# A hybrid encoder step on one Trainium2 core: the first expert pair's rows and the norms behind the experts are done by other engines

## The chip, the cores and the metric

The kernel runs on one core of one Trainium2 chip. The metric is the device time of one execution in microseconds (us); a kernel's time is the median of its runs. One engine each: TensorE (PE in the profile, its weight loads PEld), VectorE (DVE), ScalarE (ACT), GpSimd (POOL), and SyncE (SP), which here only issues DMAs.

## What is computed

One inference step of a two-layer encoder on 256 prompt and 32 sample tokens (T = 288) of width D = 1024. Layer 0 mixes tokens with RWKV-7, layer 1 with forgetting attention; each layer ends with a mixture of 16 experts, of which every token takes two from one group. Each sub-layer is closed by a norm:

```python
x = _layer_norm(ALPHA * x + gt1 * y, p['ln_g'][l, 0], p['ln_b'][l, 0])
h = x * (1 + sc2) + sh2
y = _hmoe(h, p['rg_w'][l], p['rg_b'][l], p['re_w'][l], p['re_b'][l],
          p['exp_wg'][l], p['exp_wu'][l], p['exp_wd'][l])
x = _layer_norm(ALPHA * x + gt2 * y, p['ln_g'][l, 1], p['ln_b'][l, 1])

def _layer_norm(z, g, b):
    mu = jnp.mean(z, -1, keepdims=True)
    var = jnp.mean(jnp.square(z - mu), -1, keepdims=True)
    return (z - mu) * lax.rsqrt(var + LN_EPS) * g + b

def _hmoe(h, comb, wg, wu, wd):   # comb: (token, expert), two weights per token, the rest 0
    hid = jax.nn.silu(jnp.einsum('nd,edf->nef', xf, wg)) * jnp.einsum('nd,edf->nef', xf, wu)
    hid = hid * comb[:, :, None]
    return jnp.einsum('nef,efd->nd', hid, wd)
```

Everything is float32.

## The kernel before

Activations lie feature-major: 8 tiles (KT) of 128 features by 288 tokens. The program of each engine is written out in order, and engines wait for each other through counting semaphores; an engine does nothing past a wait that is not met.

**Order of a layer.** Token mixer, its output projection, `layer_norm(0)` (or 2), `moe`, `layer_norm(1)` (or 3). Norms 0 and 2 are the even ones, norms 1 and 3, behind the experts, the odd ones. After norm 1 TensorE runs `project(4)` (L1118) on the new X; after norm 3 only Y is written out.

**Experts.** The router's choices are turned on DVE into `place` (L1595) and into four selection matrices SEL, one per group of four experts (`select`, L1598). TensorE multiplies SEL with token numbers and weights (`tables(g)`, L960), DVE makes the index table TBL of it (`table(g)`, L1607). Meanwhile the token-major rows `htok` have gone to `hbuf` in HBM (L560). The 16 experts run as 8 pairs of 64 + 64 row slots. The rows of a pair are fetched by GpSimd with an indirect DMA from `hbuf` (`fetch(p)`, L2245) into `xsel[p % 2]`, turned by TensorE (`step_t`, L1010, 8 transposes), copied by ACT to `xselT` (L2000), multiplied with gate and up weights (`step_u`, L1018, 32 instructions for an expert), multiplied by DVE (L1675), turned (`step_h`), copied by DVE (L1678), multiplied with the down weights (`step_d`, L1031, 16 instructions), scaled by DVE into `ysel` and scattered by GpSimd to `zbuf` (L2237).

The first pair is different: `first_rows` (L1001) gathers it with matmuls of `htok` and SEL[0], 8 tiles x 3 token blocks, 48 instructions, straight into the turned form. On TensorE `first_rows`, `tables(0)`, the counts (L1049) and `tables(1)` stand before the first `step_u`; `tables(2)` and `tables(3)` follow the first and second one, and `step_t(1)` the second. GpSimd fetches pairs 1 and 2, then writes the six places scatters (`places`, L2218, L2224), then fetches pair 3, and pair p + 4 once pair p + 2 is turned.

**Expert weights.** 3 MB for an expert, five slots. Five experts are loaded ahead. The rest go through SP in order (L561 to L570): gate/up of expert e + 5 when the gate/up product of e is done, and after each second one the down weights of two, which wait for a down product (`dn_mm`, L566).

**The norm behind the experts.** When all scatters have landed, ACT and SP read both choices of every token back (`rows_back`, L474; halves h = 0 and 1 with semaphores z_in0, z_in1). DVE adds the two choices in four quarters of 256 features (L1734 for two blocks of 128 tokens, L1735 for the last 32 tokens). TensorE transposes each tile (3 instructions of L628, two of 128 tokens and one of 32), DVE forms Z = ALPHA x + gate y from it (`residual`, L1479, L1492), ACT squares Z (L1964). In the odd norms GpSimd adds up Z (L2200), and TensorE adds the squares itself: `add_squares` (L923, two instructions of 288 columns) for tile k - 2 behind the transposes of tile k. In the even norms DVE adds up Z (L1486) in `residual` and GpSimd the squares, and TensorE has four matmuls at the end, one pair on each sum and on each last tile. The mean is read by ACT (L1966); DVE centers (L1507) beside GpSimd (L2205), makes the reciprocal deviation (L1516 to L1518) and scales.

**Filler.** `spin(bank, n)` (L630) runs n matmuls of 288 columns whose result nobody reads (each is two instructions, float32).

## Time and profile before

| | us |
|---|---|
| median of 3 runs | 1046.03 |
| lowest, highest | 1041.26, 1055.11 |
| the profiled execution | 1048.08 |
| its span, first to last instruction | 1046.4 |
| TensorE busy | 917.7 |
| DVE, ACT, GpSimd busy | 327.6, 232.0, 177.2 |

The profile is of one execution. Its times are counted from the start of the span. "Busy" of TensorE counts pipelined matmuls and is not work at the peak. The chain is the work that ended last, followed back from the last instruction.

### The profile page before, as it was taken

The numbers are of one execution on the slowest core, as the hardware profiler recorded it, in microseconds if no ns is written. First come the engines' busy times: TensorE is split into PE (matmuls) and PEld (weight loads), VectorE is DVE, ScalarE is ACT, GpSimd is POOL, SyncE is SP. The second block draws the span as 40 slices with busy tenths as digits, with TensorE's granted clock in tenths as the row PEclk, the third lists the DMA queues.
The fourth block names the chain that finished last, engine by engine and source line by source line (L and its number), as shares of the span: only waits on it lengthen the run. The fifth ranks groups of instructions, "written<-read, shape, count | busy, mean of one in ns | idle before, by whom it ended". The sixth has DMA issues, their size and how long they took to land.

```text
span 1046.4 us, 19214 instructions
## 1 busy us (share of the span) xinstructions
PE 917.7 (88%) x8268; PEld 627.0 (60%) x8268; DVE 327.6 (31%) x841; ACT 232.0 (22%) x528; POOL 177.2 (17%) x230
## 2 busy tenths in 40 slices
PE   2799999889988989999787899898899989997874
PEld 0477667869876757655354567554467757553442
DVE  0523341535425454211123301221221354211134
ACT  0312225223215041111001332221222131110004
POOL 0100002011542151221031110000000233211122
PEclk9899989999998998999996999899889998999996
DMA  9742221340246931799959454555646724899931
GB/s 385 322 152 89 81 81 48 127 163 4 85 173 271 387 139 57 277 425 423 424 194 369 194 189 179 195 196 214 243 164 234 322 97 182 328 424 421 383 110 46
DMA packets 28773, 230.14 MB, mean 220 GB/s; under 512 B 6590, under 2 KB 7006, under 8 KB 13552
## 3 DMA queue, kind: packets, MB, share of 16 engines
q1 hardware_dynamic: 19200, 208.66, 49.8%
q0 software_dynamic: 7776, 15.50, 4.2%
q10 hardware_dynamic: 1712, 4.75, 1.3%
q8 instruction: 66, 1.08, 0.4%
q14 instruction: 19, 0.16, 0.0%
HBM read 222.16 MB, written 16.32 MB: 228 GB/s over the span
## 4 chain that ended last, share of the span: by engine, by line
PE 68%; DMA 19%; DVE 5%; issue 3%; ACT 2%; POOL 1%; SPq 1%; ACTq 0%; POOLq 0%; DVEq 0%
PE ps L646 21%; PE ps L984 10%; DMA arena<-in_w 8%; DMA arena<-in_experts 6%; PE ps L772 5%; PE ps L667 5%; PE ps L1040 4%; PE ps L628 3%; PE ps L779 3%; DMA arena<-zbuf 2%; PE ps L1005 2%; DMA ring<-in_w 2%; PE ps L1154 2%; PE ps L970 1%; PE ps L925 1%
## 5 line engine op out<-in xcount | busy, mean ns | idle before, releaser
L646 PE MATMUL ps<-arena,ring 128*128 128x288 f32 x896 | 230.9, 420 | 11.5 <-DVE arena L1471 3.8
L646 PEld LDWEIGHTS ps<-arena,ring 128*128 128x128 f32 x896 | 173.9, 196 | 68.9 <-issue 17.1
L984 PE MATMUL ps<-arena 128*64 128x256 f32 x960 | 118.6, 404 | 18.0 <-DMA arena<-in_experts 12.6
L984 PEld LDWEIGHTS ps<-arena 128*64 128x64 f32 x960 | 75.0, 146 | 60.8 <-DMA arena<-in_experts 17.8
L667 PE MATMUL ps<-arena,csil 128*32 128x512 f32 x256 | 40.1, 756 | 36.8 <-DMA arena<-in_w 36.8
L772 PE MATMUL ps<-arena 64*64 64x64 f32 x1888 | 63.8, 221 | 4.3 <-issue 3.2
L772 PEld LDWEIGHTS ps<-arena 64*64 64x64 f32 x1888 | 60.3, 137 | 10.2 <-issue 8.5
L628 PEld LDWEIGHTS ps<-con,arena 128*128 128x128 f32 (+3 forms) x270 | 34.5, 149 | 45.5 <-issue 26.6
L628 PE MATMUL ps<-con,arena 128*128 128x128 f32 (+3 forms) x270 | 52.5, 309 | 10.2 <-DVEq L1737 6.3
L1040 PE MATMUL ps<-arena 128*64 128x512 f32 x208 | 58.4, 598 | 0.8 <-DVE arena L1678 0.8
L2003 ACT ACTIVATE arena<-ps 128x128 f32<-128x128 f32 x36 | 10.0, 277 | 208.8 <-PE ps L984 208.8
L633 PE MATMUL ps<-con 128*128 128x288 f32 x170 | 43.1, 408 | 2.1 <-DVE arena L1682 2.1
L1678 DVE COPY arena<-ps 128x128 f32<-128x128 f32 x36 | 10.5, 292 | 107.9 <-PE ps L628 107.6
L1931 ACT ACTIVATE arena<-ps 128x512 f32<-128x512 f32 x44 | 26.2, 597 | 79.2 <-PE ps L772 59.0
L1868 ACT ACTIVATE arena<-ps 128x288 f32<-128x288 f32 x40 | 16.1, 407 | 124.3 <-PE ps L646 124.3
L667 PEld LDWEIGHTS ps<-arena,csil 128*32 128x32 f32 x256 | 7.7, 125 | 58.1 <-issue 31.8
L1682 DVE TENSOR_SCALAR arena<-ps,TBL 128x512 f32<-128x512 f32 x32 | 22.6, 747 | 62.4 <-PE ps L1040 62.4
L1964 ACT ACTIVATE arena<-arena 128x288 f32<-128x288 f32 x32 | 14.2, 443 | 124.5 <-DVEq L1496 124.5
L633 PEld LDWEIGHTS ps<-con 128*128 128x128 f32 x170 | 31.8, 190 | 12.3 <-issue 3.9
L2237 POOL DMA_INDIRECT zbuf<-arena,TBL x16 | 16.1, 1005 | 127.5 <-DVE arena L1682 127.5
L1492 DVE SCALAR_TENSOR_TENSOR arena<-ps,mod,arena 128x256 f32<-128x256 f32 x64 | 20.6, 364 | 48.8 <-PE ps L646 36.8
L1315 DVE SCALAR_TENSOR_TENSOR arena<-arena,vec 128x288 f32<-128x288 f32 x48 | 21.6, 515 | 45.0 <-PE ps L646 44.0
(306 smaller groups left out, 1270.3 us busy)
## 6 DMA issues: line engine op xcount, KB each, us to landing
arena<-in_experts SPq DMA_DIRECT2D x30, 2048.0 KB, 20.6
ring<-in_w SPq DMA_DIRECT2D x24, 2048.0 KB, 8.4
arena<-in_w SPq DMA_DIRECT2D x16, 2048.0 KB, 13.3
arena<-in_experts SPq DMA_DIRECT2D x30, 1024.0 KB, 19.3
ring<-in_experts SPq DMA_DIRECT2D x6, 2048.0 KB, 19.8
ring<-in_experts SPq DMA_DIRECT2D x6, 1024.0 KB, 16.5
arena<-in_lora SPq DMA_DIRECT2D x1, 2560.0 KB, 40.8
hbuf<-arena SPq DMA_DIRECT2D x4, 512.0 KB, 3.2
```

Of the source, the lines that this page charges most:

```text
L628: return nc.tensor.transpose(out, in_, ident[0:n, 0:n])
L633: mm(ps[:, bank, 0:T], ident, con[:, 0:T], start=True, stop=True)
L646: last = mm(ps[:, tile % 4, 0:T], wslot[j][:, k, o * P:(o + 1) * P], rhs_at(k), start=k == 0, stop=k == KT - 1)
L667: last = mm(ps[32 * q:32 * q + 32, ADA_BANK[turn], :], c2[:, 2 * j + k, :], w[:, k, q, :], start=j == 0 and k == 0, stop=j == ADA_TURN - 1 ...
L772: last = mm(o, lhs[r, k, :], rhs[r, k, :], start=True, stop=True)
L779: last = mm(ps[r, bank, k * 64:(k + 1) * 64], lhs[r, k, :], rhs[r, k, :], start=n == 0, stop=n == len(terms) - 1)
L984: last = mm(ps[64 * j:64 * j + 64, 2 + b, 0:256], x(k), ewgu[slot][:, k, j * 256:(j + 1) * 256], start=k == 0, stop=k == KT - 1)
L1005: last = mm(ps[:, k // 4, k % 4 * P:(k % 4 + 1) * P], htok[0:n, i, k * P:(k + 1) * P], SEL[0][0:n, i * 4 * C:i * 4 * C + 2 * C], start=i = ...
L1040: last = mm(ps[HALF[b], 4 + n, :], hidT[b][:, f * C:(f + 1) * C], ewd[(2 * p + b) % NSLOT][:, f, n * 512:(n + 1) * 512], start=f == 0, sto ...
L1315: last = V.scalar_tensor_tensor(cut((11 + n % 3) * ACOL + k * T, T), XX[:, k, :], v(f"mu{i}", k), Hh[:, k, :], ALU.mult, ALU.add)
L1682: return V.tensor_scalar(y, ps[:, 4 + b, :], w.bitcast(F32), None, ALU.mult)
L1931: ins = Ac(B[dst], src, ACT.Copy, scale=-1.0 if product == "Bt" else 1.0)
```

## The change

1. `first_rows` is gone. Pair 0 is fetched like the others; `xsel` and `xselT[0]` move into the place of `htok`, `ysel` to a place of its own. On TensorE the two groups of table products and the counts come first, then three filler matmuls and `step_t(0)`; `step_t(1)` stands before the second `step_u` instead of behind it. GpSimd fetches pairs 0 and 1, writes the places, then fetches 2 and 3.
2. In the odd norms DVE adds the first two quarters of the choices and GpSimd the other two; DVE adds up Z in `residual`, GpSimd adds up the squares, and TensorE's end is that of the even norms.
3. The filler before the transposes of the odd norms (24 matmuls) and before `project(4)` (5) is gone.

```diff
-            ysel = [cut(at_rows + n * D, D) for n in range(2)]
-            xselT = [take(D) for _ in range(2)]
-            xsel = [ring[:, ECOL + n * D:ECOL + (n + 1) * D] for n in range(2)]
+            xsel = [cut(at_rows + n * D, D) for n in range(2)]
+            xselT = [cut(at_rows + 2 * D, D), take(D)]
+            ysel = [take(D) for _ in range(2)]
...
@@ TensorE, layer_norm and moe @@
-                if n % 2:
-                    add_squares(n, KT - 2)
...
-                if not n % 2:
-                    pe.wait_ge(s["ln_ssum"], n // 2 + 1)
-                    mm(ps[:, 5, 0:T], co("mean"), ssum, start=True, stop=False)
-                add_squares(n, KT - 1).then_inc(s["ln_var"], 1)
+                pe.wait_ge(s["ln_ssum"], n + 1)
+                mm(ps[:, 5, 0:T], co("mean"), ssum, start=True, stop=False)
+                pe.wait_ge(s["ln_sq"], KT * (n + 1))
+                mm(ps[:, 5, 0:T], co("mean"), acts(SQB[n])[:, KT - 1, :], start=False, stop=True)\
+                    .then_inc(s["ln_var"], 1)
...
-                pe.wait_ge(s["sel_ready"], 4 * layer + 1)
-                first_rows()
                 tables(0)
                 for i, n in enumerate(TOK):
                     last = mm(ps[:, 7, 448:464], ones[0:n, :], mask[0:n, i, :], start=i == 0, stop=i == 2)
                 last.then_inc(s["cnt_mm"], 1)
                 tables(1)
+                spin(2, 3)
+                step_t(0)
                 for e in range(NE):
                     step_u(e)
                     if e < 2:
                         tables(2 + e)
                     if e:
                         step_h(e - 1)
-                    if e == 1:
-                        step_t(1)
-                    if e % 2 == 0 and e:
+                    if e % 2 == 0:
                         if e + 2 < NE:
                             step_t(e // 2 + 1)
-                        step_d(e // 2 - 1)
+                        if e:
+                            step_d(e // 2 - 1)
...
-                spin(6, 24)
                 for k in range(KT):
                     c = layer * KT + k
                     if k % 2 == 0:
-                        pe.wait_ge(s["zsum"], 4 * layer + k // 2 + 1)
+                        pe.wait_ge(s[("zsum", "zsum2")[k // 4]], 2 * layer + k % 4 // 2 + 1)
...
                     last.then_inc(s["zt_mm"], 1)
-                    if k > 1:
-                        add_squares(2 * layer + 1, k - 2)
...
-            spin(6, 5)
             project(4, lambda k: X[:, k, :], ...)
@@ DVE, residual @@
                 for k in range(KT):
-                    if k > 1 and not n % 2:
+                    if k > 1:
                         did(V.tensor_tensor(zsum_, Z[:, 0, :] if k == 2 else zsum_, Z[:, k - 1, :], ALU.add))
@@ DVE, moe @@
-                for q in range(4):
+                dve.wait_ge(s["z_in0"], 48 * (layer + 1))
+                for q in range(2):
                     c = slice(q * 256, (q + 1) * 256)
-                    dve.wait_ge(s[f"z_in{q // 2}"], 48 * (layer + 1))
@@ ACT, moe @@
                 step_t(0)
                 for e in range(NE):
                     step_u(e)
-                    if e == 1:
-                        step_t(1)
-                    if e % 2 == 0 and 0 < e < NE - 2:
+                    if e % 2 == 0 and e + 2 < NE:
                         step_t(e // 2 + 1)
@@ GpSimd, layer_norm and moe @@
             def layer_norm(n):
-                total, x, ready, done = (zsum_, Z, "z_ready", "ln_sum") if n % 2 else (ssum, Q, "ln_sq", "ln_ssum")
+                if n % 2:
+                    pool.wait_ge(s["z_in1"], 48 * (layer + 1))
+                    for q in range(2, 4):
+                        c = slice(q * 256, (q + 1) * 256)
+                        ch.did(Pl.tensor_tensor(zin[:, 0:2, 0, c], zin[:, 0:2, 0, c], zin[:, 0:2, 1, c], ALU.add))
+                        ch.link(Pl.tensor_tensor(zin[0:TS, 2, 0, c], zin[0:TS, 2, 0, c], zin[0:TS, 2, 1, c], ALU.add))
+                        pool.sem_inc(s["zsum2"], 1)
                 for k in range(1, KT - 1):
-                    pool.wait_ge(s[ready], KT * n + k + 1)
-                    ch.link(Pl.tensor_tensor(total, x[:, 0, :] if k == 1 else total, x[:, k, :], ALU.add))
-                pool.sem_inc(s[done], 1)
+                    pool.wait_ge(s["ln_sq"], KT * n + k + 1)
+                    ch.link(Pl.tensor_tensor(ssum, Q[:, 0, :] if k == 1 else ssum, Q[:, k, :], ALU.add))
+                pool.sem_inc(s["ln_ssum"], 1)
...
                 def fetch(p):
                     pool.wait_ge(s["tbl_ready"], 4 * layer + p // 2 + 1)
-                    if p > 2:
+                    if p >= 2:
                         pool.wait_ge(s["xt_mm"], 2 * (p0 + p - 1))
...
-                for p in range(1, 3):
+                for p in range(2):
                     fetch(p)
                 places()
-                fetch(3)
+                for p in range(2, 4):
+                    fetch(p)
```

## Rows read from the trace of the kernel before

**Rows 1.** the page's part 4, chain by engine, share of the span.

```profile
PE 68%; DMA 19%; DVE 5%; issue 3%; ACT 2%; POOL 1%; SPq 1%; ACTq 0%; POOLq 0%; DVEq 0%
```

**Rows 2.** the chain in order of time, first layer's experts: start us, us, what.

```profile
397.85 8.51 PE ps L1005 x48
...
406.36 1.70 PE ps L970 x12
...
411.94 5.40 PE ps L984 x32
...
425.09 1.09 ACT arena L2000 x2
...
426.27 5.10 PE ps L984 x32
431.37 1.13 PE ps L628 x9
...
440.28 3.67 PE ps L984 x32
```

**Rows 3.** timeline, second layer's experts: start us, us, engine, line, operation [idle before].

```profile
857.33 8.51 PE L1005 MATMUL ps<-arena 128*128 128x128 f32 x48 [0.20 <-DVE arena L1602]
...
870.39 6.60 PE L984 MATMUL ps<-arena 128*64 128x256 f32 x32
```

**Rows 4.** timeline of SP's queue behind the first down product, both layers.

```profile
436.13 1.45 SPq L540 DMA_DIRECT2D arena<-in_experts  x2
...
894.35 0.80 SPq L540 DMA_DIRECT2D arena<-in_experts  x2
```

**Rows 5.** the chain in order of time, end of the first layer's expert loads.

```profile
487.30 30.52 DMA arena<-in_experts
```

**Rows 6.** windows: us, each engine's busy us, TensorE clock, DMA share, GB/s.

```profile
409.00:412.00 3.00, 3.00 (x15) 2.92 (x16) 0.98 (x2) 0.00 (x0) 1.14 (x1) 0.50 0.12 15
432.00:434.00 2.00, 2.00 (x13) 0.89 (x13) 0.15 (x1) 1.08 (x2) 0.63 (x1) 1.00 0.02 6
```

**Rows 7.** timeline of the norms behind the experts, first and second layer.

```profile
556.47 0.69 DVE L1734 TENSOR_TENSOR arena<-arena 128x512 f32<-128x512 f32 x1 [12.65 <-DMA arena<-zbuf]
...
561.13 0.64 DVE L1492 SCALAR_TENSOR_TENSOR arena<-ps,mod,arena 128x256 f32<-128x256 f32 x2 [0.16 <-DVE arena L1735]
562.01 0.64 DVE L1492 SCALAR_TENSOR_TENSOR arena<-ps,mod,arena 128x256 f32<-128x256 f32 x2 [0.24 <-DVE arena L1492]
...
576.27 0.41 ACT L1966 ACTIVATE lnw<-ps 128x288 f32<-128x288 f32 x1 [2.74 <-PE ps L916]
...
1014.89 0.69 DVE L1734 TENSOR_TENSOR arena<-arena 128x512 f32<-128x512 f32 x1 [13.06 <-DMA arena<-zbuf]
...
1031.05 0.41 ACT L1966 ACTIVATE lnw<-ps 128x288 f32<-128x288 f32 x1 [0.86 <-PE ps L916]
```

**Rows 8.** groups by form, DVE and GpSimd: busy us, mean ns | idle before.

```profile
L1492 DVE SCALAR_TENSOR_TENSOR arena<-ps,mod,arena 128x256 f32<-128x256 f32 x32 | 15.5, 484 | 48.8 <-PE ps L646 36.8 <-PE ps L628 10.5 <-DVE arena L1492 1.2
...
L1486 DVE TENSOR_TENSOR lnw<-lnw,arena 128x288 f32<-128x288 f32 x10 | 4.6, 459 | 2.5 <-DVE arena L1492 2.5
...
L2163 POOL TENSOR_TENSOR arena<-arena,con 128x512 f32<-128x512 f32 x5 | 6.4, 1271 | 4.9 <-DVE arena L1400 4.8
L2224 POOL DMA_INDIRECT tbl<-ENT,SLOT x12 | 11.6, 967 | 7.1 <-DVEq L1640 4.1 <-issue 3.1
```

**Rows 9.** timeline of GpSimd, the first gather of the first layer.

```profile
409.96 1.14 POOL L2232 DMA_INDIRECT ring<-hbuf,TBL  x1 [20.11 <-DVEq L1617]
```

**Rows 10.** the gathers' line L2232, issue to landing.

```profile
DMA to landing us min/median/max: 2.7/6.3/14.8
```

**Rows 11.** the centering adds' line L1507 on DVE, duration ns min/median/max.

```profile
L1507 DVE TENSOR_TENSOR arena<-arena,lnw x20: 394/453/1051, 375.0 to 1037.3; 128x288 f32<-128x288 f32 x20
```

**Rows 12.** the chain in order of time, the projection behind the first layer.

```profile
582.72 5.81 PE ps L646 x16
...
628.22 31.05 PE ps L646 x128
```

More of the change, by code:

```diff
@@ L455, in build @@
             xt_act hid_ready ht2_mm ht2_ready dn_mm y_dve z_scat0 z_scat1 o_in0 o_in1 o_in2 o_in3 oidx o_idx o_gath0 o_gath1 o_xt_mm o_xta o_gu o_silu o_hid o_ht_mm o_ht o_dn
-            o_ydve o_scat o_over z_in0 z_in1 zsum zt_mm zt_free
+            o_ydve o_scat o_over z_in0 z_in1 zsum zsum2 zt_mm zt_free
             fw_in attn_small f_mm f_act f_neg f_scan nf_ready kv_out logf_out g_in0 g_in1 att_mm att_dve att_act
@@ L972, in tables @@
                     last.then_inc(s["sel_mm"], 1)
+                tables(0)
+                for i, n in enumerate(TOK):
+                    last = mm(ps[:, 7, 448:464], ones[0:n, :], mask[0:n, i, :], start=i == 0, stop=i == 2)
+                last.then_inc(s["cnt_mm"], 1)
+                tables(1)
                 def rows_in(x, b):
@@ L999, in moe @@
                 n0, p0 = layer * NE, layer * NPAIR
[L1001 to L1008 removed]
                 def step_t(p):
[L1012 removed]
+                    pe.wait_ge(s[f"gath{p % 2}"], 16 * ((p0 + p) // 2 + 1))
                     for k in range(KT):
@@ L1043, in step_d @@
                     last.then_inc(s["dn_mm"], 1)
-                pe.wait_ge(s["sel_ready"], 4 * layer + 1)
-                first_rows()
-                tables(0)
-                for i, n in enumerate(TOK):
-                    last = mm(ps[:, 7, 448:464], ones[0:n, :], mask[0:n, i, :], start=i == 0, stop=i == 2)
-                last.then_inc(s["cnt_mm"], 1)
-                tables(1)
+                spin(2, 3)
+                step_t(0)
                 for e in range(NE):
```

12 lines of the change are left out of this document (removed).

## Prediction

> **What bounds the kernel now.** I read the chain by engine first: TensorE holds two thirds of it, DMA a fifth [rows 1]. A change pays where TensorE, or what feeds it, is late, and each stage is read for itself. In each layer the change touches the start of the experts and the norm behind them.
>
> The start of the experts, first layer, as the chain in order of time has it [rows 2]: at 397.85 DVE's choices are there and TensorE gathers the first pair's rows by matmul (48 instructions, 8.51 us). Behind it come the table products of group 0 (1.70), then the counts and the products of group 1 (408.06 to 411.94, 3.88), and only then the first gate/up. So 14.1 us stand between the choices and the first expert. In the second layer it is 857.33 to 870.39, 13.1 us [rows 3], which leaves 2.85 for the counts and group 1.
>
> Behind it, DMA. The loads for freed slots go through SP in order, and after two of them SP waits for the first down product: its next load goes out at 436.13, and at 894.35 in the second layer [rows 4]. The end of the stage is a load that stands 30.52 us in the queue, until 517.82 [rows 5]; but just before 436 the DMA engines had run dry, with a share of 0.02 at 432 to 434 [rows 6]. So all later loads queue behind that first down product, and the stage's end moves with it: what counts is the stretch from 397.85 to 436.1 (38.2 us) and 857.33 to 894.3 (37.0).
>
> The norm behind the experts, read in the timeline: DVE adds the two choices from 556.47, takes the first tile at 561.13, and ACT reads the mean at 576.27, 19.8 us after the start; second layer 1014.89 to 1031.05, 16.2 us [rows 7]. DVE's tiles waited 10.5 us in all for the transposes (L628) [rows 8]: between one tile's transposes and the next TensorE adds a tile of squares.
>
> **Part one: the first pair.** Removed: 8.51 us from the front. Behind the choices now come group 0 (1.70), counts and group 1 (2.85 to 3.88) and six filler instructions of 288 columns, 0.24 each as in the projection (31.05/128 [rows 12]), 0.49 at 1.2 GHz. The clock is 0.50, so 1.2 GHz, at 409 to 412, just behind the small products [rows 6]. TensorE is through 6.0 to 8.5 us after the choices. Beside it runs the new chain: group 0 done at 1.7; from the end of that product (408.06) to the issue of GpSimd's gather (409.96 [rows 9]) 1.9, DVE's table in it; then the landing, 2.7 us after issue at best, 6.3 in the median, 14.8 at worst [rows 10]. The long ones ran beside expert loads; here none runs, since the first is released by the first gate/up, so I take 2.7 to 3.7: rows there at 6.3 to 7.3. Both chains meet near 7.3. Then eight transposes, about 1.0 (nine in 1.13), twice that at 1.2 GHz, and ACT's second copy, 0.54 (two in 1.09) and 0.2 of hand-over [rows 2]. The first gate/up starts 9 to 12 us after the choices; I take 10.
>
> The first gate/up took 5.40 and 6.60; at full clock it is 3.67 [rows 2, 3]. The excess, 1.73 and 2.93, is 3.5 and 5.9 us at half speed. Filler and transposes are now dense work ahead of it, so the clock should be back somewhat earlier in it: 5.2. It ends at 15.2 instead of 19.5 and 19.6: 4.3 us gained per layer.
>
> From there to the first down product the same instructions run in another order. The second pair's transposes ahead of the second gate/up hide ACT's copy, 1.2 us bare before (425.06 to 426.27), but uncover the hidden block's turn and DVE's copy, for which ACT's 0.54 and a transpose of 0.13 are the nearest rows, with hand-overs 0.8 to 1.1: 0.1 to 0.4 gained, none counted beyond 0.1. In the first layer the third gate/up took 5.10 instead of 3.67 [rows 2], behind that 1.2 us hole; I count half of the 1.43. Together 5.0 and 4.3 us (bounds 2 and 6.5 each). From SP's load behind the down product on, the shift is carried in full.
>
> Queues. GpSimd now issues two gathers, then six places scatters (0.97 each [rows 8], some 7.5 us with gaps), and then the gathers of pairs 2 and 3, which used to stand before the scatters or wait for later transposes. The scatters start some 8 us earlier than before, with DVE's entries, so pair 2's gather goes out about 18 us after the choices and is read at about 29: 10 us of room against a median of 6.3; free, and some 4 us at the worst landing. Pair 1's is read at 17 and issued at 5. Its bytes, at most 128 rows of 4 KB (0.5 MB, about 1 us), fall ahead of the first down product, where DMA runs dry anyway. SP's order is unchanged.
>
> **Part two: the norm behind the experts.** DVE had 4.66 us for four quarters (556.47 to 561.13); two are 2.33. GpSimd adds the other two: 1.27 for a 128x512 add [rows 8] and no more than that for the small piece, so 4 to 5 us in all, and DVE needs them only at its fifth and seventh tile: hidden. But the engines hold each other up: DVE's centering adds took 453 ns in the median and up to 1051, beside GpSimd's of the same stretch [rows 11]. I take 3.0 for DVE's two quarters (2.3 to 3.8). The Trainium skill (GPSIMD Engine Reference, Key points) says that GpSimd shares its SBUF interfaces with VectorE and contends with DVE instructions that have two SBUF inputs. That speaks against this change, whose adds on both engines are such; the trace agrees with the 1051.
>
> Then eight tiles on DVE, 0.88 each (561.13 to 562.01 [rows 7]), from the third on with a running add of Z, 0.46 less some overlap [rows 8]: 2 x 0.88 + 6 x 1.3 + 0.1 = 9.7. TensorE has one tile's transposes to do in that time (about 0.4, or 0.7 at 1.2 GHz), so DVE leads. The last tile is ready 12.7 us after the start, the mean is read 0.8 to 1.3 later: 13.9. Gained 19.8 - 13.9 = 5.9 and 16.2 - 13.9 = 2.3 us (within 1.5 each way). GpSimd's squares follow each tile and are not slower than DVE; the last two matmul pairs of the variance stand behind the mean as in the first norms.
>
> The filler goes too. The 24 pairs hid behind the DMA: free by itself. But TensorE comes to the projection with a hole behind it. There the first tile's 16 instructions took 5.81, against 3.9 at full clock [rows 12]; all at 1.2 GHz they take 7.8. I charge 1.0 us (0 to 2.5, the rest for tiles behind). No matmul follows the last norm. The projection's weights are asked for at the landing, 20 us ahead.
>
> **Sum:** -5.0 - 4.3 - 5.9 - 2.3 + 1.0 = -16.5 us. The profiled execution took 1048.08 (span 1046.4), so 1031.6 by it; it lies 2 us above the median shown, 1046.03, which gives 1029.5. I say 1030.5.
>
> **Rivals.**
> (a) All at its good end: clock kept through the tables, rows there after 2.7 us, no hold-up on DVE: -6 and -5.5 at the experts, -6.5 and -3.5 in the norms, projection free, some -22: 1024.5. For: each piece has a row; against: the first gate/up was slowed by the clock in both layers. 0.14.
> (b) The first gather lands like the median one, 6.3: first gate/up at 12.6 in both layers, 2.6 later each: 1036. For: no cover but the filler; against: empty queues. 0.10.
> (c) DVE and GpSimd hold each other up at every add: ten adds of DVE in each norm take 0.6 more, 12 us in all: 1042. For: the 1051; against: the squares start just behind DVE's running add. 0.08.
> (d) Slower, by the clock. Place: from the tables to the end of the second gate/up. Small products and a wait stand where dense matmuls stood; if 1.2 GHz then lasts through both gate/ups, a layer pays 2.5 (start at 12.5), 2.0 (first gate/up 7.2), 1.7 (group products), 1.0 (transposes) and 3.7 (second gate/up), 10.9, and two of them 21.8: 1052. It turns the sign from 16.5 us on, some 33 us of additional lower clock. For: 0.50 at 409 to 412. Against: dense work brought the clock back after 3.5 and 5.9 us. 0.05. The Trainium skill (TensorE: Matmul & The Clock Gate, What's actually happening) calls the throttled state the default that activity releases; by that rule taking filler out invites (d). The trace bears out the fall, not a long stay.
>
> **How the numbers follow.** The sum has 0.63. The range, 1022 to 1041, takes in (a), (b) and the near half of (c). Faster by over 2% (below 1025.1) are most of (a) and the sum's lower tail: 0.18; slower by over 2% is only a worse (d): 0.02; within 2%: 0.80. 2% is about what a measurement of this kernel can tell from no change.
>
> **What would show it.** Right: first gate/up about 10 us after the choices, no 48-matmul group; SP's load behind the first down product about 33 us after the choices in both layers; the mean about 14 us after DVE's first add in both norms, its tiles no longer waiting for L628. Wrong: pair 0's transposes waiting for the gather beyond 8 us; DVE adds of 0.7 us and more all along; a projection whose first tile takes 8 us.

## The result, and the profile after

The changed kernel takes 1043.03 us (median of 20 runs, 1033.78 to 1054.06) beside 1048.91 us for the kernel before on the same chip (20 runs, 1038.59 to 1057.76). The ratio is 0.9935, with a 95% interval from 0.991 to 0.996: 6.8 us less (4.2 to 9.4). The ratio, here and below, goes by the fast runs, those not more than 1.5% above the fastest of their kernel. Forecast were 16.5 us less, 1030.5 us, with a range from 1022 to 1041; the measured time lies outside it. The sign was right and the size 2.4 times too large.

The profiled execution has a span of 1041.5 us (before 1046.4). Its chain by engine stands as before, TensorE two thirds and DMA a fifth, with a little more for DVE [rows 1]:

```profile
PE 66%; DMA 19%; DVE 7%; issue 4%; ACT 2%; POOL 1%; SPq 1%; ACTq 0%; POOLq 0%; DVEq 0%
```

Timeline of TensorE in the changed kernel, first layer's expert start (start us, us, engine, line, operation, [idle before]); against [rows 2]:

```profile
398.72 2.39 PE L961 MATMUL ps<-VAL,arena 128*128 128x6 f32 x12 [0.36 <-DVE arena L1580]
401.04 1.57 PE L967 MATMUL ps<-arena,con 128*128 128x16 f32 x6
402.54 3.00 PE L961 MATMUL ps<-VAL,arena 128*128 128x6 f32 x12
405.47 3.25 PE L630 MATMUL ps<-con 128*128 128x288 f32 x6
408.51 1.66 PE L625 MATMUL ps<-con,arena 128*128 128x128 f32 x8
410.95 3.67 PE L981 MATMUL ps<-arena 128*64 128x256 f32 x32 [0.78 <-ACT arena L1979]
...
425.01 3.67 PE L981 MATMUL ps<-arena 128*64 128x256 f32 x32 [1.22 <-DVE arena L1656]
```

The 48-matmul group is gone. TensorE never waits between the choices (398.72) and the transposes of pair 0 (408.51): its own small products and fillers fill 9.8 us, and the first gate/up starts 12.2 us after the choices, not 10. In the second layer (choices at 854.81) the transposes start after 8.8 us and the gate/up after 10.8. The windows say why (us, PE busy, PEld, DVE, ACT, POOL, TensorE clock, DMA share, GB/s):

```profile
398.00:400.00 2.00, 1.64 (x10) 1.24 (x9) 1.54 (x2) 0.00 (x0) 0.00 (x0) 0.88 0.00 0
404.00:406.00 2.00, 2.00 (x8) 1.92 (x8) 0.39 (x2) 0.00 (x0) 1.17 (x2) 0.50 0.32 84
408.00:410.00 2.00, 2.00 (x10) 1.65 (x8) 1.64 (x12) 0.39 (x1) 0.00 (x0) 0.56 0.05 20
410.00:412.00 2.00, 1.22 (x12) 0.91 (x12) 1.73 (x9) 1.98 (x3) 1.21 (x2) 1.00 0.01 4
```

The stretch at 1.2 GHz, about 409 to 415 before ([rows 6] show its start), has moved ahead to the tables. Twelve table instructions that take 1.77 at full clock take 3.00 there, and a filler instruction 0.54. The first gate/up itself ran at full clock, 3.67 us in both layers.

What counts is SP's load behind the first down product, in both layers; against [rows 4]:

```profile
433.44 1.03 SPq L537 DMA_DIRECT2D arena<-in_experts  x2
...
889.90 0.88 SPq L537 DMA_DIRECT2D arena<-in_experts  x2
```

It comes 34.7 and 35.1 us after the choices (398.72; 854.81), where it was 38.2 and 37.0: 3.5 and 1.9 us gained of 5.0 and 4.3 forecast. (Below, "+55.3" is a time behind the start of the norm's reciprocal ahead of the experts, which each profile has: norm 0's in the first layer, norm 2's in the second.) In the second layer the third gate/up ran into a second stretch at 1.2 GHz, which the first layer was spared:

```profile
880.00:882.00 2.00, 2.00 (x16) 1.48 (x14) 0.00 (x0) 0.00 (x0) 0.00 (x0) 0.70 1.00 424
882.00:884.00 2.00, 2.00 (x13) 1.36 (x11) 0.00 (x0) 0.00 (x0) 0.00 (x0) 0.50 0.84 338
```

The norm behind the first layer's experts, timeline, against [rows 7]:

```profile
553.52 1.26 POOL L2177 TENSOR_TENSOR arena<-arena 128x512 f32<-128x512 f32 x1 [9.39 <-DMA arena<-zbuf]
553.79 1.54 DVE L1713 TENSOR_TENSOR arena<-arena 128x512 f32<-128x512 f32 x1 [13.50 <-DMA arena<-zbuf]
554.75 1.16 POOL L2178 TENSOR_TENSOR arena<-arena 32x256 f32<-32x256 f32 x1
555.25 0.93 DVE L1714 TENSOR_TENSOR arena<-arena 32x256 f32<-32x256 f32 x1
...
556.33 1.56 DVE L1713 TENSOR_TENSOR arena<-arena 128x512 f32<-128x512 f32 x1 [0.15 <-DVE arena L1714]
...
557.82 0.94 DVE L1714 TENSOR_TENSOR arena<-arena 32x256 f32<-32x256 f32 x1
...
558.91 0.64 DVE L1470 SCALAR_TENSOR_TENSOR arena<-ps,mod,arena 128x256 f32<-128x256 f32 x2 [0.16 <-DVE arena L1714]
...
570.21 0.41 ACT L1945 ACTIVATE lnw<-ps 128x288 f32<-128x288 f32 x1 [1.02 <-PE ps L910]
...
570.93 1.17 PE L915 MATMUL ps<-arena,con 128*128 128x288 f32 x2
...
572.70 0.94 DVE L1495 TENSOR_SCALAR lnw<-lnw 128x288 f32<-128x288 f32 x1
573.68 1.95 DVE L1496 RECIPROCAL lnw<-lnw 128x288 f32<-128x288 f32 x1
```

DVE's two quarters take 5.12 us (553.79 to 558.91), more than its four did (4.66): an add of 128x512 takes 1.54 beside GpSimd's instead of 0.69. The mean is read 16.4 us after DVE's start, not 13.9. In norm 3 DVE starts at 1011.38 and the mean is read at 1026.17, after 14.8. GpSimd's half of the rows landed first there, and its first add started 1.6 us before DVE's.

Behind the mean, norm 1 lost another 0.74 us: its reciprocal starts 3.47 us after the mean is read, where it was 2.73. The same stretch before, same view:

```profile
576.07 0.65 PE L925 MATMUL ps<-arena,con 128*128 128x288 f32 x2
...
578.53 0.43 DVE L1517 TENSOR_SCALAR lnw<-lnw 128x288 f32<-128x288 f32 x1
```

In the changed kernel TensorE's last pair of products for the variance stands behind the mean's. At half clock it takes 1.17 us. Then DVE's next instruction starts 0.2 us later, and the one behind it (L1495) takes 0.94 instead of 0.43. Of the 30 norms behind experts with this end in the profiles, 21 have the pair at 1.16 or 1.17 and the reciprocal 3.46 to 3.48 after the mean; the other nine have it at 1.00 or less and 2.71 to 2.73.

For what follows I count stages from the start of one norm's reciprocal to the next one's. "Load" is SP's load behind the first down product, "add" the first add of the choices on either engine.

| us | before | after |
|---|---|---|
| layer 0: reciprocal of norm 0 to load | 58.8 | 55.3 |
| to add | 179.2 | 175.4 |
| add to reciprocal of norm 1 | 22.5 | 20.2 |
| reciprocal of norm 1 to that of norm 2 | 256.9 | 259.6 |
| layer 1: reciprocal of norm 2 to load | 58.4 | 56.6 |
| to add | 179.0 | 176.5 |
| add to reciprocal of norm 3 | 18.9 | 19.2 |

The fourth line holds the attention, which the change doesn't touch. Over the later profiles it lies between 253.9 and 269.5 us, so its scatter alone is larger than the effect looked for.

### The profile page after: what moved, and what is told of

Same layout as the page of the kernel before. It is cut to its first block, busy times and chain, and to the rows that moved or that the text cites. A ratio compares the mean times of both kernels' runs of the same rounds, so it can differ in the third digit from the quotient of the medians.

```text
span 1041.5 us, 18838 instructions
## 1 busy us (share of the span) xinstructions
PE 879.5 (84%) x8070; PEld 598.6 (57%) x8070; DVE 333.3 (32%) x845; ACT 232.0 (22%) x528; POOL 187.6 (18%) x240
## 4 chain that ended last, share of the span: by engine, by line
PE 66%; DMA 19%; DVE 7%; issue 4%; ACT 2%; POOL 1%; SPq 1%; ACTq 0%; POOLq 0%; DVEq 0%
PE ps L643 21%; PE ps L981 9%; DMA arena<-in_w 8%; DMA arena<-in_experts 6%; PE ps L769 5%; PE ps L664 5%; PE ps L1028 4%; PE ps L625 3%; PE ps L776 3%; DMA arena<-zbuf 2%; DMA ring<-in_w 2%; PE ps L961 2%; PE ps L1132 2%; PE ps L782 1%; PE ps L925 1%
## 5 line engine op out<-in xcount | busy, mean ns | idle before, releaser
L643 PE MATMUL ps<-arena,ring 128*128 128x288 f32 x896 | 230.3, 419 | 13.4 <-ACT arena L1953 5.3
L643 PEld LDWEIGHTS ps<-arena,ring 128*128 128x128 f32 x896 | 173.6, 196 | 71.0 <-issue 19.2
L981 PEld LDWEIGHTS ps<-arena 128*64 128x64 f32 x960 | 75.7, 143 | 61.3 <-issue 19.7
L625 PE MATMUL ps<-con,arena 128*128 128x128 f32 (+3 forms) x398 | 69.3, 305 | 39.9 <-DVEq L1716 36.0
L625 PEld LDWEIGHTS ps<-con,arena 128*128 128x128 f32 (+3 forms) x398 | 48.1, 150 | 74.8 <-DVEq L1716 37.8
L1028 PE MATMUL ps<-arena 128*64 128x512 f32 x208 | 58.4, 598 | 0.8 <-DVE arena L1656 0.8
L1656 DVE COPY arena<-ps 128x128 f32<-128x128 f32 x36 | 10.5, 292 | 107.9 <-PE ps L625 107.6
L1910 ACT ACTIVATE arena<-ps 128x512 f32<-128x512 f32 x44 | 26.2, 597 | 78.2 <-PE ps L769 59.1
L1132 PE MATMUL ps<-arena,ring 128*128 128x288 f32 x128 | 33.4, 415 | 0.0
L1979 ACT ACTIVATE arena<-ps 128x512 f32<-128x512 f32 x36 | 19.7, 595 | 51.9 <-PE ps L625 43.9
## 6 DMA issues: line engine op xcount, KB each, us to landing
arena<-in_w SPq DMA_DIRECT2D x16, 2048.0 KB, 13.5
arena<-in_experts SPq DMA_DIRECT2D x30, 1024.0 KB, 19.2
```

The lines of the kernel that those rows point to most:

```text
L625: return nc.tensor.transpose(out, in_, ident[0:n, 0:n])
L643: last = mm(ps[:, tile % 4, 0:T], wslot[j][:, k, o * P:(o + 1) * P], rhs_at(k), start=k == 0, stop=k == KT - 1)
L981: last = mm(ps[64 * j:64 * j + 64, 2 + b, 0:256], x(k), ewgu[slot][:, k, j * 256:(j + 1) * 256], start=k == 0, stop=k == KT - 1)
L1028: last = mm(ps[HALF[b], 4 + n, :], hidT[b][:, f * C:(f + 1) * C], ewd[(2 * p + b) % NSLOT][:, f, n * 512:(n + 1) * 512], start=f == 0, sto ...
L1132: last = mm(ps[:, b, 0:T], wslot[j][:, k, o * P:(o + 1) * P], X[:, k, :], start=k == 0, stop=k == KT - 1)
L1910: ins = Ac(B[dst], src, ACT.Copy, scale=-1.0 if product == "Bt" else 1.0)
```

## The experiments

The first four split the change in its halves, undid GpSimd's share, and put the fillers back. Each was timed (12 runs) beside the kernel before (1049.57 us, 35 runs).

**e1: the expert half alone.** All hunks of the expert start in `moe` (pair 0 fetched, the new order on TensorE and GpSimd), none of the norms'.

> The expert half of the change alone; both later norms stay as before. Theory S (the shifts read at the four stages of the profile after: -3.5 and -1.9 us at the loads behind the first down product, -2.6 and -1.3 us at the reciprocals of norms 1 and 3): 4 to 5.5 us under before, ratio 0.995 to 0.996. Rival T (what the experts gain is given back behind the last load, where the tails of both layers were about 1 us longer): 1 to 2 us under before, ratio 0.998 to 0.999.

Measured: ratio 0.9952 (0.9908 to 0.9996), 5.0 us less. The stages repeat: load at +55.2 and +57.0, add at +175.7 and +178.3. Theory S stands in the middle; T's range (1 to 2 us) lies inside the interval (0.4 to 9.7) too. Its norms, as before in code, took 22.5 and 22.4 us. So the 18.9 us of norm 3 in the profile before was the one short norm of four, with a granted clock of 0.68 over the 16 us from the first add:

```profile
1015.00:1031.00 16.00, 12.51 (x43) 7.89 (x44) 9.09 (x24) 3.54 (x8) 4.75 (x6) 0.68 0.01 2
```

and here 0.57 over 20 us:

```profile
1015.00:1035.00 20.00, 16.12 (x44) 9.81 (x44) 9.12 (x24) 3.90 (x9) 4.76 (x6) 0.57 0.00 0
```

That the old norm goes by TensorE's clock is read from these rows, not tested; the changed one took 19.0 to 19.9 us in norm 3 in every profile with this end.

**e2: the norm half alone.** All hunks of the norms and fillers, the expert start as before.

> The norm half alone (GpSimd adds two quarters and the squares, DVE the tiles, TensorE no squares and no filler products); the experts start as before. Theory S: 3 to 4 us under before, ratio 0.996 to 0.997, with DVE's two quarters in norm 1 again at 4 to 5 us beside GpSimd's. Rival N (the norms gain nothing, the whole 6.8 us is the experts'): within 1 us of before, ratio 0.999 to 1.001.

Measured: 0.9994 (0.9962 to 1.0026), 0.6 us less. The profile has norm 1 at 20.2 us, so its gain of 2.4 is there, and DVE's two quarters at 1.47 and 1.56 for the large adds. In time rival N is nearer, though theory S's 3 to 4 us still lie inside the interval, at its end. The profile's loads behind the first down product stood at +60.9 and +63.5, 2 and 5 us later than before, in a part that this edit doesn't touch.

**e3: DVE adds all four quarters.**

```diff
@@ TensorE @@
-                        pe.wait_ge(s[("zsum", "zsum2")[k // 4]], 2 * layer + k % 4 // 2 + 1)
+                        pe.wait_ge(s["zsum"], 4 * layer + k // 2 + 1)
@@ DVE @@
-                dve.wait_ge(s["z_in0"], 48 * (layer + 1))
-                for q in range(2):
+                for q in range(4):
                     c = slice(q * 256, (q + 1) * 256)
+                    dve.wait_ge(s[f"z_in{q // 2}"], 48 * (layer + 1))
@@ GpSimd, layer_norm: its two quarters gone @@
...
```

> The changed kernel with all four quarters of the two expert choices added by DVE; GpSimd keeps the squares. Theory C (DVE and GpSimd hold each other up in these adds, so that the share given to GpSimd is worth almost nothing): DVE's adds go back to 0.69 and 0.41 us, two quarters take 2.3 us and four 4.7 us, the whole within 1 us of the changed kernel. Rival A (the share was worth its whole price, four quarters of DVE being late for the transposes of tiles 4 to 7): 1.5 to 4 us slower than the changed kernel.

Measured: 1041.17 us, 0.9929 (0.9888 to 0.997). Its norm 1, DVE's timeline:

```profile
551.46 0.69 DVE L1713 TENSOR_TENSOR arena<-arena 128x512 f32<-128x512 f32 x1 [12.98 <-DMA arena<-zbuf]
552.07 0.40 DVE L1714 TENSOR_TENSOR arena<-arena 32x256 f32<-32x256 f32 x1
...
556.12 0.48 DVE L1470 SCALAR_TENSOR_TENSOR arena<-ps,mod,arena 128x256 f32<-128x256 f32 x1 [0.16 <-PE ps L625]
...
570.14 1.95 DVE L1496 RECIPROCAL lnw<-lnw 128x288 f32<-128x288 f32 x1
```

The adds are back at 0.69 and 0.40, four quarters take 4.66 us, and the reciprocal starts 18.7 us after the first add instead of 20.2 (norm 3: 18.3 instead of 19.2). Theory C holds, and more than it said: in its stage the share given to GpSimd is a loss. From the first add to the reading of the mean it is 15.96 us instead of 16.69. That is 0.7 us of the 1.5; the other 0.75 is the step behind the mean described above, whose long form this execution was spared in both norms. In the later profiles with this edit (e10 to e12) norm 1 has the long form again and takes 19.4, against 20.2. Rival A falls by the stage; the two ratios, 0.6 us apart with an interval of some 5 us either way, can't tell it.

**e4: the fillers back.** `spin(6, 24)` ahead of the transposes and `spin(6, 5)` ahead of `project(4)`.

> The changed kernel with both fillers back (24 products ahead of the transposes of the later norms, 5 ahead of the projection behind norm 1); its output is the same. Theory P (the change's norm is slower than forecast partly because TensorE stands at half clock through norms 1 and 3): start to reciprocal of norm 1 falls by 1 to 2 us, and the kernel by 1 to 3 us. Rival D (the norm goes at DVE's pace and TensorE's clock doesn't matter there): within 0.7 us of the changed kernel.

Measured: 1039.92 us, 0.9918 (0.9883 to 0.9952). The fillers do hold the clock up to the norm, but not in it. Windows of e4:

```profile
552.00:554.00 2.00, 0.00 (x0) 0.00 (x0) 0.94 (x1) 0.00 (x0) 1.17 (x1) 1.00 0.19 36
556.00:560.00 4.00, 3.22 (x13) 1.69 (x12) 3.36 (x7) 0.51 (x2) 1.78 (x2) 0.50 0.99 418
```

and of the changed kernel:

```profile
552.00:554.00 2.00, 0.00 (x0) 0.00 (x0) 0.21 (x1) 0.00 (x0) 0.48 (x1) 0.50 0.16 43
556.00:560.00 4.00, 2.92 (x11) 1.68 (x11) 3.44 (x6) 0.20 (x1) 2.39 (x2) 0.50 1.03 422
```

Norm 1 took 20.2 us and norm 3 19.2, to 0.02 us what they were: theory D in the norm, since the fillers left the clock in it as it was. The time, 1.8 us less by the two ratios, is nearer to theory P's 1 to 3 us, but within the intervals.

The next four looked at the expert start, with one execution each, profiled; one of the kernel before beside them took 1051.64 us. Their times can't be told from chance; what they say is in their rows.

**e5: pair 1's transposes behind the second gate/up again.**

```diff
-                    if e % 2 == 0:
+                    if e == 1:
+                        step_t(1)
+                    if e % 2 == 0 and e:
...
@@ ACT: its copies in the same order @@
```

> The changed kernel with the transposes of pair 1 behind the second gate/up product, where they stood before. Theory Q (moving them ahead of it is what costs the second layer 1.3 us between the second gate/up product and the first down product, and their signal comes 4 us late): second load's release falls by about 1 us in both layers (from +43.7 and +43.4 us behind the reciprocal to about +42.7), the load behind the first down product by 0.5 to 1.5 us (from +55.3 and +56.5). Rival W (the order of the two is worth nothing, what counts is the sum of TensorE's work up to the first down product): that load stays within 0.3 us in layer 0.

The second load goes out at +42.9 and +42.7 as expected, but the load behind the first down product at +57.8 and +57.4, later than in the changed kernel: the third gate/up fell into 1.2 GHz in both layers (6.32 and 6.10 us, 3.67 at full clock). The changed kernel has such loads too where its clock falls there (+57.1 to +57.8 in e4, e9, e13 and e14), so the later load is the clock's and not shown to be the order's. Theory Q's gain isn't seen; the order gives 0.8 us at the second load and nothing behind it. The kernel took 1042.13 us.

**e6: ten fillers behind the first tables.** `spin(2, 5)` behind `tables(0)`, none ahead of `step_t(0)`.

> The changed kernel with ten filler products directly behind the first tables and none ahead of the transposes of pair 0. Theory K (the first gate/up product was late because TensorE's clock stood at half from the tables to the first transposes, though TensorE was busy): the granted clock rises earlier, the first expert load is released 1 to 2 us earlier than +38.0. Rival G (the gather's rows set that point): release within 0.4 us of +38.0. If the clock stays at half all the same, the fillers cost 2 us.

The first load goes out at +37.5 and +38.5. The ten fillers took 5.17 us at half clock; the clock came back by the second tables and fell again. Behind the second gate/up TensorE stood idle three times with nothing in the profile that it waited for ("issue"); from 420 to 426 the DMA share was 0.67 to 0.79:

```profile
421.25 0.48 PE L961 MATMUL ps<-VAL,arena 128*128 128x6 f32 x3 [0.24 <-issue]
422.67 0.48 PE L961 MATMUL ps<-VAL,arena 128*128 128x6 f32 x3 [0.94 <-issue]
424.08 0.81 PE L961 MATMUL ps<-VAL,arena 128*128 128x6 f32 x6 [0.94 <-issue]
```

The load behind the first down product came at +59.1 and +59.9, the kernel took 1053.4. Theory K falls as a cure: filling by hand at this place cost more than it gave in this profile.

**e7: no filler ahead of pair 0's transposes.** `spin(2, 3)` dropped.

> The changed kernel without the six filler products ahead of the transposes of pair 0. If the gather's rows set the start (rival G): transposes start at the same 10.0 us behind the choices, first gate/up slower by 0 to 2 us from a longer time at half clock. If TensorE's own work set it: transposes start 0.3 to 2 us earlier.

```profile
404.80 3.00 PE L961 MATMUL ps<-VAL,arena 128*128 128x6 f32 x12
408.72 1.97 PE L625 MATMUL ps<-con,arena 128*128 128x128 f32 x8 [0.92 <-DMA arena<-hbuf,TBL]
```

Here TensorE does wait for the gather, 0.92 us, and the transposes start 7.7 us after the choices (400.99) instead of 9.8. So the rows are there at 7.7, and in the changed kernel TensorE's own work set the start. But the first gate/up then ran partly at half clock (5.67 us), the first load went out at +38.0 and +38.3 as before, and the next ones at +57.8 and +57.9. What the start gained (1.8 us at the first gate/up), the clock took. (The kernel's 1056.34 us has 268 us between the reciprocals of norms 1 and 2, which this edit doesn't touch.)

**e8: the first hidden rows turned ahead of the tables of pairs 6 and 7.** The 1.22 us wait of the third gate/up for DVE's L1656 (first timeline above) is DVE's copy standing behind `table(3)`.

```diff
@@ TensorE @@
-                    if e < 2:
-                        tables(2 + e)
+                    if e == 0:
+                        tables(2)
                     if e:
                         step_h(e - 1)
+                    if e == 1:
+                        tables(3)
@@ DVE: the same, table(3) behind step_h(0) @@
```

> The changed kernel with the transpose and the copy of the first hidden rows ahead of the tables of pairs 6 and 7, on TensorE and on DVE. Theory H (TensorE's wait of 1.2 us ahead of the third gate/up product, which DVE's copy of the hidden rows ends behind the table's four instructions, sets the first down product): the load behind the first down product 1 to 1.5 us earlier, at about +54.2 and +55.3. Rival: DVE's copy was hidden by something else that is late, and the load stays within 0.3 us.

Measured: load at +53.8 and +53.5, the kernel 1036.84 us. The wait is gone, the third gate/up took 3.67 in both layers and no second stretch at 1.2 GHz follows in either. At the load the first layer gained the 1.5 us of theory H; the second gained 3.1, the wait and the clock. At the first add of the choices it is 1.9 and 1.5 us: of the second layer's gain only half had arrived by then, in this one execution.

Then four timed kernels, beside the kernel before (1048.81 us, 29 runs).

**e9: the changed kernel again.**

> The changed kernel itself, beside the three that follow: 0.992 to 0.995 of before; first add to reciprocal 20.2 us in norm 1 and 19.2 in norm 3 again if these are set by the engines' pace. Of the load behind the first down product a second reading: +55.3 us (layer 0) where the third gate/up product runs at full clock, +57 where the clock falls under it.

1041.73 us, 0.9936 (0.9892 to 0.998): the result repeats. Norms 20.2 and 19.8. The load came at +57.3 in the first layer, with the third gate/up mostly at half clock (6.59 us), and at +54.0 in the second, at full clock. Expected were +57 and +55.3. Here the first expert load went out at +36.5 and +36.1, 1.5 and 1.9 us earlier than in the first profile (see the last section), about what the +54.0 is early. Windows of the first layer:

```profile
424.00:426.00 2.00, 0.78 (x5) 0.60 (x7) 1.34 (x6) 0.00 (x0) 0.00 (x0) 0.71 0.98 340
426.00:430.00 4.00, 4.00 (x20) 2.40 (x19) 0.00 (x0) 0.00 (x0) 0.00 (x0) 0.50 0.96 370
```

**e10: e3 and e8 together.**

> The changed kernel with DVE adding all four quarters and the first hidden rows turned ahead of the tables of pairs 6 and 7. Theory C+H (both edits act where they were seen to act): load behind the first down product +53.8 and +53.5 us, first add to reciprocal 18.7 and 18.3 us, in all 4 to 6 us under the changed kernel. Rival: the stretch behind the last load grows by what the start gains (it did by about 1 us in each layer), and the whole is 1.5 to 3 us under the changed kernel.

1039.13 us, 0.9912 (0.9874 to 0.995). The load at +53.0 and +52.7, the third gate/up without a wait:

```profile
422.74 0.33 PE L625 MATMUL ps<-con,arena 128*128 128x128 f32 x1
422.91 1.67 PE L961 MATMUL ps<-VAL,arena 128*128 128x6 f32 x12
424.51 3.67 PE L981 MATMUL ps<-arena 128*64 128x256 f32 x32
```

Reciprocal to reciprocal is 192.7 and 193.4 us, against 198.8 and 195.4 of e9 on the same chip, 8 us by the stages, 2.6 by the medians (the intervals overlap). Part of the 8 is not the edits': e9's first layer had its third gate/up at half clock. Against the first profile the load is 2.4 and 3.9 us earlier, of which some 1.5 in each layer is the earlier first load that e9 has too; at the first add of the choices 2.2 and 1.4 us are left. In the second layer the stretch from the load to the add is 122.4 us, the longest of all, so the rival is not excluded.

**e11: e10 with both groups of fillers.**

> The kernel e10_both with the two groups of fillers back. With GpSimd adding, the fillers kept the clock at full up to the norm and yet left norm 1 at 20.2 us, since DVE and GpSimd set its pace. Theory D (DVE's 1.25 us a tile sets the pace here too, whatever the clock): norms 18.7 and 18.3 us, within 1 us of e10_both. Rival P (with the adds short, TensorE's transposes and mean products at half clock are what is left): norms 0.5 to 1.5 us shorter each.

1035.21 us over 6 runs, 0.9881 (0.9826 to 0.9935): the lowest median of the study, 12.5 us below the kernel before by the ratio. The norms are 19.4 and 19.0 us where e10 had 19.4 and 18.3, so theory D holds in them and P's shorter norms are not seen; the kernel, though, is 3.9 us below e10 by the medians, not within 1 us, with overlapping intervals. What the fillers may give is behind norm 1: the projection's first tile took 4.72 us in e11,

```profile
575.03 4.72 PE ps L643 x16
```

6.89 in e10 and 5.62 in the changed kernel:

```profile
576.38 6.89 PE ps L643 x16
```
```profile
577.41 5.62 PE ps L643 x16
```

and its x128 group starts 48.1 us behind the reciprocal in e11, 50.3 in e10. In e4, though, the first tile took 6.25 with the same fillers; that they always help is not shown.

**e12: the norm half alone with DVE adding all quarters.** e2 with the edit of e3.

> The norm half alone with DVE adding all four quarters (squares by GpSimd, sum of tiles by DVE, no squares and no fillers on TensorE); the experts start as before. Theory C: first add to reciprocal 18.7 us in norm 1 (before 22.5) and 18.3 in norm 3 (before 18.9 or, at half clock, 22.4), so 4 to 7 us under before, ratio 0.993 to 0.996. Rival R (what the norm half gains is lost at the experts, where the norm half alone showed its loads 2 to 5 us late in both layers): within 1.5 us of before.

1052.01 us, 1.0000 (0.9955 to 1.0046). The profile has norms of 19.4 and 19.0 us, and loads at +59.0 and +56.9, so rival R's late loads are not seen in the stages (this execution has 269.5 us between the reciprocals of norms 1 and 2). The time is nearer to what R said, within 1.5 us of before; a gain of 4 us is still in the interval, one of 7 is not.

**e13, e14, e15: a known delay at each place.** The stages promise more than the times give. So 13 instructions whose result changes nothing went ahead of DVE's quarters in norm 1 (e13) and norm 3 (e14), and 40 small ones ahead of the choices of layer 0 (e15). The kernel before took 1052.38 us beside them (29 runs), and the three 1052.43, 1052.87 and 1051.77 (12 runs each).

```diff
+                if layer == 0:
+                    for _ in range(13):
+                        link(V.tensor_tensor(zin[:, 0:2, 1, 0:256], zin[:, 0:2, 1, 0:256], zin[:, 0:2, 1, 0:256], ALU.max))
```

> The changed kernel with 13 idle instructions on DVE (each the greater of a value and itself) ahead of its first quarter of the choice in norm 1, about 10 us by 0.7 to 0.8 us each. Theory F (a microsecond at norm 1 is one of the whole): the time grows by the delay less what GpSimd's half and the transposes lose nothing by, 8 to 10 us over the changed kernel, 1.002 to 1.004 of before. Rival A (the stages behind wait for loads that were issued ahead of the norm): 3 to 7 us, and reciprocal of norm 1 to reciprocal of norm 2, 256 to 259.6 us in the changed kernel, falls by the rest.

> The same delay in norm 3, behind which only the output follows. Both theories: the time grows by the delay seen at the reciprocal of norm 3, 8 to 10 us over the changed kernel. It is the measure for the other two.

> The changed kernel with 40 idle instructions on DVE ahead of the choices of layer 0, about 10 us by 0.25 us each. Theory F (the loads behind the first down product are bound by the DMA queues from there to the last load, so the whole shifts): the first down product's load, the read of the rows and the time are all later by the delay, 9 to 11 us. Rival B (the loads already under way fill part of it, or the tail behind the last load shrinks): the read of the rows is later by 2 us less than the load.

| | seen in its stage, us later than the changed kernel | ratio to before (interval) | time over the changed kernel |
|---|---|---|---|
| e13 | reciprocal of norm 1: 29.0 - 20.2 = 8.9 | 1.0025 (0.9993 to 1.0057) | 9.4 |
| e14 | reciprocal of norm 3: 29.0 less 19.0 to 19.9 = 9.1 to 10.0 | 1.0014 (0.9983 to 1.0046) | 8.3 |
| e15 | load: 67.8 less 55.2 to 57.8 = 10.0 to 12.6 | 1.0029 (0.9995 to 1.0063) | 9.9 |

(The last column is the ratio less 0.9935, times 1048.9.) A microsecond at each of the three places is about one of the whole, with some 4 us either way on each time. Theory F fits all three. Rival B falls: in e15 the read of the rows was late by as much as the load (10.2 to 13.5 us at the first add). Rival A is not excluded: e13's profile has 253.9 us between the reciprocals of norms 1 and 2, the shortest of all, 2 to 6 us less than the changed kernel's 256.0 and 259.6, as A expects; but that execution was the fastest of e13's 12, 5 us below their median, and the median shows no such gift. In e13 DVE's delay itself was 12.0 us and only 8.9 of it reached the reciprocal, because GpSimd was through when DVE's quarters came:

```profile
553.24 11.98 DVE L1713 TENSOR_TENSOR arena<-arena 128x512 f32<-128x512 f32 x13 [13.65 <-DMA arena<-zbuf]
565.25 0.69 DVE L1716 TENSOR_TENSOR arena<-arena 128x512 f32<-128x512 f32 x1
...
566.41 0.69 DVE L1716 TENSOR_TENSOR arena<-arena 128x512 f32<-128x512 f32 x1 [0.15 <-DVE arena L1717]
```

Alone, the two quarters take 2.3 us: 2.8 of the 5.12 are the hold-up by GpSimd.

## Why the prediction was wrong in size

The forecast had the places and the direction right. Three terms failed: the small products and fillers ahead of the first gate/up, the missing wait ahead of the third one, and DVE's two quarters.

**Start of the experts, -5.0 and -4.3: found -3.5 and -1.9.** The step "TensorE is through 6.0 to 8.5 us after the choices" failed; it took 9.8 us (8.8 in the second layer). I had priced the fillers at both clocks, but group 0, the counts and group 1 at their rows of before, 1.70 and 2.85 to 3.88, read behind 48 dense matmuls and partly at full clock. In the changed kernel the small products themselves stand at 1.2 GHz: 2.39 + 1.57 + 3.00, and 3.25 for the fillers (1.77 + 1.22 + 3.00 + 3.25 in the second layer, where the clock fell a little later). So the first load went out 17.4 and 16.4 us after the choices (416.14; 871.24) instead of 19.5 and 19.7: 2.1 and 3.3 us gained of 4.3. The gather was sized almost rightly (rows there at 7.7 in e7, 6.3 to 7.3 forecast), as was its queue: pair 2's went out at 418.13, 19.4 us after the choices (18 forecast), and nothing waited for it. The first gate/up was forecast at 5.2 us, partly at half clock; the rows have it at 3.67, all at full clock, and yet SP's load went out 5.2 and 5.7 us behind its start. That the forecast number came out is luck: by these rows the clock wasn't its cause, and what the cause was is open.

The second part of the miss is "none counted beyond 0.1" between the first gate/up and the first down product. The new order has a wait of 1.22 us of its own ahead of the third gate/up, for DVE's copy behind `table(3)`, in place of the one for ACT. From the first load to the one behind the first down product it took 17.3 us in the first layer (before 18.8), with the third gate/up at full clock, and 18.7 in the second (before 17.3), with it at 5.36 us: 1.4 gained, 1.3 lost. Over seven profiles with this start (the first, e1, e3, e4, e9, e13, e14) the load lies at +55.2 to +57.8 in the first layer and, with e15's second layer, at +54.0 to +57.3 in the second; with the old one over three (before, e2, e12) at +58.8 to +60.9 and +56.9 to +63.5. Rival (d) named the clock over the small products rightly; that it would stay low through both gate/ups, and so its price, not. Ten fillers ahead of the second group didn't cure it (e6).

**From the load on "the shift is carried in full": right in the main.** In the first layer the add came 3.8 us later before than after, 2.5 in the second; in e15, whose load was 10.0 to 12.6 later, it came 10.2 to 13.5 later (188.8 less 175.3 to 178.6). The stretch from load to add itself scatters, from 118.2 to 121.3 us in the first layer and from 119.5 to 122.4 in the second over all profiles, so a shift of 1 to 2 us can't be followed through it.

**Norm 1, -5.9: found -3.4 at the mean, -2.4 at the reciprocal. Norm 3, -2.3: found -1.4 at the mean and +0.3 at the reciprocal.** (The mean is counted from DVE's first add, as in the forecast, the reciprocal from the first add on either engine.) The step that failed is "I take 3.0 for DVE's two quarters (2.3 to 3.8)". They took 5.12 and 3.87. In e13, where they took 2.3 and GpSimd had long finished its adds, the mean was read 13.3 us after the first of them, so the rest of the sum up to the mean stood. What norm 1 gained less at its reciprocal than at its mean is 0.3 us for GpSimd's earlier start and 0.74 for the end: "the last two matmul pairs of the variance stand behind the mean" is in the forecast, but priced at nothing. In norm 3 that end cost nothing in this profile (2.72 both times), and the 1.6 us between GpSimd's start and DVE's make the difference. Rival (c) was this mechanism with the wrong reach: it put 0.6 us on ten adds, and the runs show 0.85 on a large and 0.5 on a small add of the quarters and nothing on the tiles. There the argument against (c) held. DVE's running add (L1464) is over when GpSimd starts to add the square (L2183), and GpSimd works beside DVE's tile, which takes one operand from PSUM; all three keep their pace:

```profile
561.93 0.46 DVE L1464 TENSOR_TENSOR lnw<-lnw,arena 128x288 f32<-128x288 f32 x1 [0.24 <-DVE arena L1470]
562.31 0.64 DVE L1470 SCALAR_TENSOR_TENSOR arena<-ps,mod,arena 128x256 f32<-128x256 f32 x2
562.47 0.79 POOL L2183 TENSOR_TENSOR lnw<-lnw,arena 128x288 f32<-128x288 f32 x1 [0.53 <-ACT arena L1943]
```

The Trainium skill (GPSIMD Engine Reference, Key points) names contention for DVE instructions in a 2-port perf mode or with two SBUF inputs. The adds of the quarters, which have two such inputs, agree (1.54 us instead of 0.69); the tile, which has one operand in PSUM, was not slowed. The forecast named this and priced it at 0.7 us. In norm 3 the forecast took one reading of before for its level; the same code gave 18.9 us in one profile and 22.4 in another, with a lower granted clock.

**Projection, +1.0: found -0.2.** The first tile took 5.62, before 5.81 [rows 12]; but e10 had 6.89. Over the profiles without the fillers the second tile started 11.2 to 12.7 us behind the reciprocal, 11.4 in the kernel before, so the charge lay within what executions differ by.

**The whole.** The steps as found, -3.5, -1.9, -2.4 and -0.5 (midway for norm 3), make -8.3; the time says -6.8, with 4.2 to 9.4 as its interval. By the times of e13 to e15 none of the places loses its price on the way, to some 4 us in 10. The expert half is most of it (-5.0 alone). The norm half by itself is not told from nothing by two sets of runs (0.9994, 1.0000), though its stage is 2.4 to 3.1 us shorter in each profile; whether the rest is chance or given back in a stage of large scatter stays open. Open too is whether taking the fillers out cost something: both kernels that had them back (e4, e11) were faster than their pair without, by 1.8 and 3.3 us of ratio, neither clear of its interval.

## What to carry to other kernels

When work is shared out between DVE and GpSimd, ask whether both will read two SBUF operands at the same time: two engines on such adds took longer (5.1 us for half of the work each) than DVE alone with all of it (4.7). Price small products at both clock levels when what stands ahead of them changes, as the forecast had done for its fillers alone. Behind a reordering, look for the next wait on the same product: a copy that stood behind the same engine's table held TensorE up for 1.2 us a layer, and moving one call ahead took that away (1.5 to 3 us at the next load, 1.5 to 1.9 at the stage's end, in one execution). And look at what stands behind the last result that you priced: here 0.75 us in most norms.

## What the runs showed of the hardware

- TensorE can be busy without a gap and stand at 1.2 GHz all the same. From 400 to 408 in the changed kernel it was busy 2.00 us of each 2.00 at a granted 0.50, first with products of 6 and 16 columns, from 405.5 on with the fillers of 288. Its only wait from 394 to 400, where the clock fell, had been 0.36 us.
- Whether the clock falls a second time, under the third gate/up, differed between executions of one kernel (the changed one: first profile in layer 1, second profile in layer 0). Over the eight profiles with this start unaltered (in e15 but for the delay ahead of it) it fell in 9 of 16 such stretches. With the 1.22 us wait ahead of it gone, it fell in none of the six of e8, e10 and e11. Why it falls in one and not in another with the wait is open.
- A DVE TENSOR_SCALAR with one input (L1495) took 0.94 or 0.95 us in 21 norms and 0.36 to 0.44 in all others, beside GpSimd's three adds (L2188) each time. The long form came exactly where the instruction ahead of it had started 2.0 instead of 1.8 us behind the mean.
- In most profiles the first gate/up's followers (ACT, SP) went on 1.4 to 2.5 us behind the end that the records show for it, and in e9 to e11 at once (3.7 us behind its start). Its cause was not found; the records' ends are modelled, and only the releases are used above.
